# Combines after the experts: weighted sums moved to TensorE, modulation columns made between tiles, last normalisation on ScalarE

## The reference, cut to what matters

```
y = sum over the two chosen experts of weight * expert_output
x = layer_norm(ALPHA * x + (1 + gate_f) * y) * g + b
h = x * (1 + scale) + shift        # next layer only, its modulation
```

## Time and profile before

| | |
|---|---|
| runs, us | 2249.93, 2246.52, 2246.26 (median 2246.52) |
| the profiled execution | 2247.56 us, its span 2245.7 us |
| busy in the span | PE 83%, DVE 36%, ACT 17%, POOL 15% |
| combine after layer 0, from the store before it to the next stage | about 985 to 1034.7 us of the span |
| combine after layer 1 | about 2181 us to the end |

### The profile page before, as it was taken

How to read it: one execution, slowest core, us unless ns; L and a number is a source line. 1 busy time by engine, 2 the same in 40 slices (tenths; PEclk the granted TensorE clock), 3 DMA queues, 4 the chain that set the end, 5 groups by cost and what they waited for, 6 DMA issues and landing times. The chain is left out here.

```text
span 2245.7 us, 35420 instructions
## 1 busy us (share of the span) xinstructions
PE 1871.8 (83%) x14911; PEld 988.5 (44%) x14911; DVE 801.3 (36%) x1654; ACT 380.1 (17%) x844; POOL 335.5 (15%) x448
## 2 busy tenths in 40 slices
PE   5999999999899669954898998998996769939970
PEld 3443443434234333323765755755754534423320
DVE  0122333233332320025336546546544423240007
ACT  1010000100000111113132232333231110001211
POOL 0020110101111200021031031121021002120104
PEclk8999999999989879975898999998996789959985
DMA  9365738555350199966323123223214583068964
GB/s 337 130 213 192 259 104 290 195 181 198 112 204 36 61 390 400 397 240 214 114 86 86 47 68 102 66 65 101 71 63 123 195 233 136 19 238 304 402 245 149
DMA packets 232255, 396.66 MB, mean 177 GB/s; under 512 B 16893, under 2 KB 88197, under 8 KB 232070
## 3 DMA queue, kind: packets, MB, share of 16 engines
q1 hardware_dynamic: 226146, 372.90, 47.7%
q0 software_dynamic: 5952, 21.50, 2.6%
HBM read 300.86 MB, written 93.51 MB: 176 GB/s over the span
## 5 line engine op out<-in xcount | busy, mean ns | idle before, releaser
L552 PE MATMUL bank<-ring,hT 128*128 128x512 f32 x768 | 345.4, 600 | 3.3 <-PEq L267 2.2
L1291 PE MATMUL bank<-hT,ring 128*128 128x272 f32 x1024 | 290.8, 422 | 11.1 <-PEq L874 11.1
L552 PEld LDWEIGHTS bank<-ring,hT 128*128 128x128 f32 x768 | 142.3, 191 | 188.6 <-issue 185.9
L1291 PEld LDWEIGHTS bank<-hT,ring 128*128 128x128 f32 x1024 | 190.9, 199 | 59.0 <-issue 24.9
L2263 PE MATMUL bank<-expert_w,exp_xT 128*32 128x512 f32 x1152 | 177.6, 624 | 16.3 <-DMA expert_w<-in_moe_w_gu_dram 12.4
L2854 PE MATMUL bank<-ring,oT 128*128 128x512 f32 x384 | 173.3, 613 | 13.3 <-DMA oT<-oT_spill 12.7
L2854 PEld LDWEIGHTS bank<-ring,oT 128*128 128x128 f32 x384 | 75.0, 197 | 107.0 <-issue 93.9
L1288 PE MATMUL bank<-ring,hT 128*128 128x512 f32 x256 | 116.1, 599 | 0.0
L2263 PEld LDWEIGHTS bank<-expert_w,exp_xT 128*32 128x32 f32 x1152 | 47.5, 115 | 127.2 <-issue 122.0
L2287 PE MATMUL bank<-expert_w,exp_aT 128*32 128x512 f32 x576 | 90.1, 617 | 8.8 <-DMA expert_w<-in_moe_w_down_dram 7.4
L2357 DVE TENSOR_TENSOR exp_a<-bank,exp_sg 128x256 f32<-128x256 f32 x24 | 10.2, 424 | 224.2 <-ACT exp_sg L2340 224.2
(11 more groups left out here) (442 smaller groups left out, 2553.2 us busy)
## 6 DMA issues: line engine op xcount, KB each, us to landing
ring<-in_w_ada_dram SPq DMA_DIRECT2D x24, 2048.0 KB, 9.7
expert_w<-in_moe_w_gu_dram SPq DMA_DIRECT2D x24, 2048.0 KB, 16.7
expert_outputs<-ret_zeros SPq DMA_DIRECT2D x15, 2048.0 KB, 10.5
expert_w<-in_moe_w_down_dram SPq DMA_DIRECT2D x24, 1024.0 KB, 16.7
ring<-in_ret_w_in_dram SPq DMA_DIRECT2D x8, 2048.0 KB, 14.2
ret_Ss<-in_state_ret_dram SPq DMA_DIRECT2D x32, 512.0 KB, 5.1
out_dram<-ret_Ss SPq DMA_DIRECT2D x32, 512.0 KB, 4.0
oT<-in_moe_w_gu_dram SPq DMA_DIRECT2D x8, 2048.0 KB, 21.8
```

The costliest lines, as they stand in the source:

```text
L552: last = pe.matmul(ps[u % 2][:, :], core.hT[:, k, tok(t)], core.ring[:, w % RING, k, :], start=(k == 0), stop=(k == KD - 1))
L1291: mm = pe.matmul(ps[U % 2][:, 0:HALF], core.ring[:, w % RING, k, c * P:(c + 1) * P], core.hT[:, k, half * HALF:(half + 1) * HALF], start=( ...
```

## The change

Both combines form the weighted sum on TensorE: VectorE first makes, for each tile and each of the two experts, a diagonal matrix from the identity and the column of weights (`weight_columns`: ten operations); `weighed` then counts bank halves, which TensorE fills by two matmuls each. In `combine`, ScalarE normalises, from a centre column that GpSimd makes as a third tiny operation, VectorE multiplies by g, and for the fifth tile VectorE adds b itself. In `combine_features`, TensorE's and ScalarE's lists are put in another order, VectorE adds the modulation's bias after tile 2 and makes the columns between tiles 3 and 4, and the sample rows are applied from the PSUM banks. The diff, cut to its core:

```diff
 def combine(core, l, plan, x_from, x_to):
...
+                def deviation(t):
+                    n, v = rows(t), t % 2
+                    r.deviation(pool, t)
+                    pool.wait_ge(r.rstd_done, t + 1)
+                    pool.tensor_scalar(centre[0:n, t, :], r.mom[0:n, v, 0:1], r.rstd[0:n, v, :], -1.0, ALU.mult, ALU.mult
+                                       ).then_inc(s["centre_done"], 1)
+                deviation(0)
                 for t in range(NT):
                     if t + 1 < NT:
-                        r.deviation(pool, t + 1)
+                        deviation(t + 1)
-                    r.outputs(pool, t)
+                    if t < NPT:
+                        r.outputs(pool, t)
...
+            @block.tensor
+            def _(pe):
+                for t in range(NT):
+                    weighted_sum(pe, core, t, diag, ya, yb, s[f"got{t}"], s["diag_done"], s["y_used"], s["weighed"])
...
+                weight_columns(dve, core, plan, diag, s["diag_done"])
                 def join(t):
-                    dve.wait_ge(s["weighed"], t + 1)
-                    chain(dve.scalar_tensor_tensor(A, B, plan.weight[0:n, 1, t:t + 1], A, ALU.mult, ALU.add))
-                    r.join(dve, chain, t, [(slice(0, D), A, B)], None)
+                    dve.wait_ge(s["weighed"], 2 * (t + 1))
+                    if t >= 2:
+                        dve.wait_ge(s["normed"], t - 1)
+                        dve.wait_ge(s["centre_done"], t - 1)
+                    r.join(dve, chain, t, [(slice(c * W, (c + 1) * W), ps[2 * (t % 2) + c][0:rows(t), :],
+                                            yb[0:rows(t), t, c * W:(c + 1) * W]) for c in range(2)], taken)
+                def finish(t):
+                    x = r.x[0:rows(t), t, :]
+                    dve.wait_ge(s["normed"], t + 1)
+                    dve.wait_ge(r.vec_in, r.vec_total)
+                    if t < NPT:
+                        dve.tensor_tensor(x, x, r.g[0:rows(t), :], ALU.mult).then_inc(r.xn_used, 1)
+                    else:
+                        chain(dve.tensor_tensor(x, x, r.g[0:rows(t), :], ALU.mult))
+                        dve.tensor_tensor(x, x, r.b[0:rows(t), :], ALU.add).then_inc(s["last_done"], 1)
...
             def _(act):
                 for t in range(NT):
+                    act.wait_ge(s["centre_done"], t + 1)
+                    act.activation(X, X, ACT.Identity, bias=centre[0:n, t, :], scale=r.rstd[0:n, v, :]).then_inc(s["normed"], 1)
...
+def weight_columns(dve, core, plan, diag, done):
+    for t in range(NT):
+        n = rows(t)
+        for j in range(2):
+            dve.tensor_scalar(diag[0:n, t, j, 0:n], core.ident[0:n, 0:n], plan.weight[0:n, j, t:t + 1], None, ALU.mult
+                              ).then_inc(done, 1)
...
+def weighted_sum(pe, core, t, diag, ya, yb, got, diag_done, taken, weighed):
+    n = rows(t)
+    pe.wait_ge(diag_done, 2 * (t + 1))
+    pe.wait_ge(got, 32)
+    if t >= 2:
+        pe.wait_ge(taken, 2 * (t - 1))
+    for c in range(2):
+        for j, y in enumerate((ya, yb)):
+            last = pe.matmul(core.ps[2 * (t % 2) + c][0:n, :], diag[0:n, t, j, 0:n], y[0:n, t, c * W:(c + 1) * W],
+                             start=(j == 0), stop=(j == 1))
+        last.then_inc(weighed, 1)
...
 def combine_features(core, plan, x_from, xn_to):
...
             def _(dve):
+                weight_columns(dve, core, plan, diag, s["diag_done"])
...
                 for t in range(NT):
-                    dve.wait_ge(s["weighed"], t + 1)
-                    chain(dve.scalar_tensor_tensor(A, B, plan.weight[0:n, 1, t:t + 1], A, ALU.mult, ALU.add))
-                    chain(dve.scalar_tensor_tensor(B, gate[0:n, m, :], 1.0, A, ALU.add, ALU.mult))
+                    for c in range(2):
+                        half = slice(c * W, (c + 1) * W)
+                        dve.wait_ge(s["weighed"], 2 * t + c + 1)
+                        dve.scalar_tensor_tensor(B[:, half], gate[0:n, m, half], 1.0, ps[2 * (t % 2) + c][0:n, :], ALU.add, ALU.mult
+                                                 ).then_inc(s["y_used"], 1)
...
+                    if t == 2:
+                        dve.wait_ge(core.ada_done, 16)
+                        for n in range(13, 16):
+                            core.keep_modulation(dve, n, ps[6][:, (n - 13) * P:(n - 12) * P], res[:, n - 12, :], core.BIASES["routing"])
+                    if t == 3:
+                        columns()
-                dve.wait_ge(s["kept"], 2 * NT)
+                dve.wait_ge(s["kept"], 2 * NPT)
...
             def _(pe):
                 pe.transpose(ps[7][:, 0:2 * KD], norm_rows[:, :], core.ident[0:2 * KD, 0:2 * KD]).then_inc(s["norm_turned"], 1)
-                for n in range(13, 16):
-                    core.modulate(pe, n, ps[n - 9])
-                for t in range(NT):
-                    turn_tile(pe, core, x[:, t, :], t, (2 * (t % 2), 2 * (t % 2) + 1)).then_inc(s["turned"], 1)
+                shift(13)
+                shift(14)
+                for t in range(3):
+                    add(t)
+                turn(0)
+                shift(15)
+                add(3)
+                turn(1)
+                add(4)
+                turn(2)
                 for n in range(4):
                     last = pe.transpose(ps[7][:, n * P:(n + 1) * P], res[:, n, :], core.ident[:, :])
                 last.then_inc(s["mod_turned"], 1)
+                turn(3)
+                turn(4)
...
             def _(act):
+                scale(0)
+                for t in range(1, NPT):
                     scale(t)
+                    keep(t - 1)
                 act.wait_ge(s["mod_turned"], 1)
...
+                scale(NPT)
+                keep(NPT - 1)
                 act.wait_ge(s["cols_done"], 1)
```

More of the change, by code:

```diff
@@ L2382, in combine @@
         r = Residual(core, st, l, 1, False)
-        s = {n: st.sem(n) for n in ("steps", "y_used", "weighed")}
+        diag, centre = st.sb("diag", [P, NT, 2, P]), st.sb("centre", [P, NT, 1])
+        s = {n: st.sem(n) for n in ("steps", "y_used", "weighed", "diag_done", "centre_done", "normed", "last_done")}
         for t in range(NT):
@@ L2391, in _ @@
                 r.vectors(sp)
-                for t in range(NT):
+                for t in range(NPT):
                     r.store(sp, t, x_to)
+                sp.wait_ge(s["last_done"], 1)
+                sp.dma_start(x_to(NPT), r.x[0:NS, NPT, :]).then_inc(r.x_out, 16)
                 r.stored(sp)
@@ L2537, in _ @@
                     dve.tensor_scalar(out, out, gain[:, k, 0:1], offset[:, k, 0:1], ALU.mult, ALU.add).then_inc(s["dve_done"], 1)
-                each = lambda a: a[:, :, 1:NC].unsqueeze(3).broadcast_to([P, KD, DECB, DECL])
-                out = core.hT[:, :, SEQ:NTOK].rearrange("p k (b l) -> p k b l", l=DECL)
-                dve.tensor_tensor(out, out, each(gain), ALU.mult).then_inc(s["smp_done"], 1)
-                dve.wait_ge(s["smp_done"], 1)
-                dve.tensor_tensor(out, out, each(offset), ALU.add).then_inc(s["smp_done"], 1)
+                dve.wait_ge(s["turned"], NT)
+                for half in range(2):
+                    ks = slice(4 * half, 4 * half + 4)
+                    each = lambda a: a[:, ks, 1:NC].unsqueeze(3).broadcast_to([P, 4, DECB, DECL])
+                    out = core.hT[:, ks, SEQ:NTOK].rearrange("p k (b l) -> p k b l", l=DECL)
+                    src = ps[2 + half][:, 0:4 * NS].rearrange("p (k b l) -> p k b l", k=4, l=DECL)
+                    dve.tensor_tensor(out, src, each(gain), ALU.mult).then_inc(s["smp_done"], 1)
+                    dve.wait_ge(s["smp_done"], 2 * half + 1)
+                    dve.tensor_tensor(out, out, each(offset), ALU.add).then_inc(s["smp_done"], 1)
             @block.tensor
@@ L2547, in _, with add, turn, shift @@
                 pe.transpose(ps[7][:, 0:2 * KD], norm_rows[:, :], core.ident[0:2 * KD, 0:2 * KD]).then_inc(s["norm_turned"], 1)
-                for n in range(13, 16):
-                    core.modulate(pe, n, ps[n - 9])
-                for t in range(NT):
+                def add(t):
+                    weighted_sum(pe, core, t, diag, ya, yb, got[t], s["diag_done"], s["y_used"], s["weighed"])
+                def turn(t):
                     pe.wait_ge(s["scaled"], t + 1)
-                    if t >= 2:
-                        pe.wait_ge(s["kept"], 2 * (t - 1))
-                    turn_tile(pe, core, x[:, t, :], t, (2 * (t % 2), 2 * (t % 2) + 1)).then_inc(s["turned"], 1)
+                    if t == NPT:
+                        pe.wait_ge(s["y_used"], 2 * NPT)
+                    elif t:
+                        pe.wait_ge(s["kept"], 2 * t)
+                    turn_tile(pe, core, x[:, t, :], t, (2, 3) if t == NPT else (4, 5)).then_inc(s["turned"], 1)
+                def shift(n):
+                    core.modulate(pe, n, ps[6][:, (n - 13) * P:(n - 12) * P])
+                shift(13)
[8 more added lines that the diff above has]
```

(1 more changed line is left out.)

59 lines of the change are left out of this document (20 added, 39 removed).

## The result

| | before | after |
|---|---|---|
| median of 12 runs, us | 2244.26 | 2259.24 |
| lowest to highest | 2237.86 to 2252.75 | 2249.78 to 2265.40 |
| the profiled execution, its span | 2247.56, 2245.7 | 2265.28, 2263.3 |
| instructions | 35420 | 35605 |

The ratio on record is 1.0055, 95% interval 1.0037 to 1.0073: slower by about 12.3 us. (The two medians alone lie 15.0 us apart; all that follows goes by the ratios.) I had forecast no change, 2246.5, and the result lies above the range. The two combines did almost what I had worked out. Most of the loss is between them: in the profiles it stands in the stages from `delta_gates` on, called the delta stage here, whose instructions the change doesn't touch.

What follows compares the result with a forecast made beforehand. Both combines were taken as VectorE-bound, with TensorE first on the path in the changed first one. Minus 6.3 (last) plus 6.2 (first) came to nothing: 2246.5 us, range 2241.5 to 2251.5.

Steps and rivals of the forecast that it cites:

- Last combine, minus 6.3: Last combine: VectorE tile period falls from 9.5 to 7.4 us, last sample row at 2236.6, so 6.3 us saved.
- the middle I chose: Last combine, tile 0's first sum on TensorE: between 3.5 us at full clock and 7.0 at half, taken as 5.3.
- The contention: Last combine: GpSimd's addition of b holds VectorE's residual half, 1.5 us a tile; rival of less contention, chance 0.12.
- First combine, plus 6.2: Combine after layer 0: plus 6.1 us to tile 3's moments because sums start late, plus 0.1 in the chain behind.
- S: Combine after layer 0: when modulations 13 and 14 are done and TensorE's weighted sums start, forecast at 1003.3.
- idle time before the columns: Combine after layer 0: VectorE does nothing else for 5.0 us around deviation, scale(3), keep(2), copies and columns, ahead of tile 4.
- Nothing elsewhere: Stages outside the two combines: no term given, the sum being only minus 6.3 plus 6.2 us.
- No pause: Rival, combine after layer 0: TensorE's instruction pause doesn't recur, that combine loses 1.7 instead of 6.2, total 2242.0; chance 0.18.
- Half clock in the last combine: Rival, last combine: TensorE stays at 1.2 GHz, 7.0 us a tile, gain only 1.5, total 2251.3; chance 0.10.
- More stalls in the first combine: Rival, first combine: second instruction pause or sums at half clock, 3 to 8 us more, 2249.5 to 2254.5; chance 0.08.
- The sign: Whole kernel: no change, within about 0.2% or 4.5 us; chances same 0.58, faster 0.27, slower 0.15.
- The weight columns: Last combine, ten operations before the first gather lands: may slow a gather's issue by nothing to 0.4 us, taken as nothing.

Runs made afterwards that it cites:

- pad_real: Kernel before plus 20 small TensorE matmuls and six already-met waits in idle time ending the first combine: 2255.5 us, ratio 1.0034 to the kernel before.
- last_only: Kernel before with only the last combine changed, the combine after layer 0 left old: 2241.52 us, ratio 0.9970 to the kernel before.
- after_realigned: Whole change plus 42 small TensorE matmuls, 25 in the first combine, 17 in the stage behind: 2239.81 us, ratio 0.9984 to the kernel before.
- best42: Changed kernel with first-combine sums before modulations, columns behind tile 4, 42 small matmuls starting TensorE's list there: 2240.43 us, ratio 0.9979 to kernel before.

## Why the prediction was wrong, point by point

**The step that failed** is the first: "The combines run one after the other with everything else, each between barriers, so each has its own bound, and the two results add." The terms do add, but they are not all. The new list ahead of the delta stage moves TensorE's later instructions by 86 places, and that costs 5 to 11 us in stages that no line of the change touches (pad_real: +7.6 from that alone). In the traces packets of instructions then fall into the stores and loads of the state, and TensorE waits longer for it: its gaps there add up to 9.7 us in place of 5.6 on average. The prediction put this term at nothing and gave no reason. I even wrote "The starvation might not recur when the instructions fall otherwise" among the rivals, but only for the one pause. I never asked what else in the program depends on how they fall.

**Last combine, minus 6.3:** it shows -7.0 in the profile, and last_only -6.7. The first sum took longer than the middle I chose: VectorE began 6.5 us after TensorE did, at half clock for most of it, where I had 5.3. The contention is 2.24 - 0.69 = 1.55 a tile, by my 1.5, and the period 7.1 against 7.4. One reading was wrong, though the sum doesn't rest on it: L2739 doesn't end when GpSimd's addition ends. The addition ends at 2217.66 + 3.31 = 2220.97 and L2739 at 2222.06, so the operation does nearly all of its own 1.2 us behind it.

**First combine, plus 6.2:** +7.7. Counted from the stage's first load, the sums start 19.5 us later; I had 1003.3 - 985.8 = 17.5. Behind it, moments of tile 3 at S+20.8 (S+21.0), idle time before the columns 4.19 (5.0). The last operation ends 16.0 us behind those moments (16.4). The miss is the length of the pause. That TensorE "finds no instructions to run" in it isn't shown: no packet of instructions ends it, as said above.

**Nothing elsewhere:** about +11. This is the error of the prediction; the other two add to +0.7 (from first load to last store) or +1.2 (to the end of the span), close to the nothing that I had. That they come so close is partly luck: the first lost 1.5 more than forecast, the last gained 0.7 more.

**The rivals.** No pause: it does happen, in one execution of two of after_realigned, and there the combine is 5.5 us shorter (51.0 and 56.5) where I had 4.5; but not in the two of the changed kernel that were profiled. Half clock in the last combine: only over its first sum (granted clock 0.55 over 2216.9 to 2223.2, 1.00 over 2223.2 to 2227.0). More stalls in the first combine: none. The sign went to a mechanism that I gave no chance.

**The weight columns** cost nothing: the first gather beside them was issued in 0.94 us, as the later ones were. By the Trainium skill (GPSIMD Engine Reference, section 8, Key points) VectorE operations in a two-port mode contend with GpSimd, from which I had inferred a loss of a few tenths; the trace shows none.

**What stays open:** what the rest of the difference is made of. Of the 7.4 us by which the mean delta stages differ, the waits for the state are 4.1. By the same traces TensorE's waits for VectorE are 3.1 more, which no run separates from the waits for the state, and its busy time is 1.6 more. The late instructions themselves cost no more: the gaps without a wait, those at L1468 left out, are 9.9 us on average at the position of before and 8.5 at the others. But executions of one program also differ by as much. That a packet holds up the state's transfers is read from all the traces, but no run moved the store or the load and left the instructions where they were.

**The best of these** is the old first combine with the new last one (last_only, 0.9970), with best42 (0.9979) and after_realigned (0.9984) no different from it within the intervals. best42 has the reordered first combine at the position of before, but that combine is only 0.9 us shorter than the old one there (48.0), too little to show.

## What to carry to other kernels

The number of instructions ahead of a stage can be part of that stage's cost. TensorE's instructions come in packets over the DMA engines; where they fall decides where TensorE pauses for them, and, by these traces, which of the program's own transfers take longer. So after any edit compare the stages that it does not touch, and move the position with a few matmuls in idle time before blaming the edit. Where the view says that idle time ended in no wait, look at the waits in the source and at the landings just before it. Measure each part of a change by itself; here one part gains 0.3%, the other loses 0.7%, and nearly half of that loss is not where the edit is (6.5 of 15.0 us).

## What was unexpected of the hardware

Pauses of TensorE without a wait, 0.5 to 4.2 us long, stand at one place of its instruction stream in all 16 traces (62 of 62 at place 193 of a block of 256), whichever operation is there, and end 1.2 to 1.7 us behind a packet of 16384 bytes of instructions. Where such a packet starts inside a store of two times 512 KB, the load that waits for the first half starts 3.6 to 5.3 us after the store (33 of 33); where none does, 3.3 to 3.5 (76 of 79). Twenty matmuls of 32 x 16 in idle time (2.31 us, none of it on the path) made the program 7.6 us slower, 1.0034 [1.0018, 1.0051]; 42 of them made another 0.7% faster (0.9984 in place of 1.0055). The pause in the first combine is not in every execution: 128 records took 6.31 us without it, and about 11.6 with it (992.55 to 1004.1). The delta stage of one program took 798.8 us in one execution and 811.5 in another.
